# Storing the bias lines ahead of the last modulation pieces and the first weights, x as the first transfer, squares ahead of the line copy

## The reference

```python
x = x + pool_mixer(rmsnorm(x, norm_mixer[0]), pool_w[0], pool_scale[0])   # window means 2, 4, 8, 16, then a 256x256 product a group
x = x + swiglu(rmsnorm(x, norm_ffn[0]), w_gate_up[0], w_down[0])          # D_FF 2816
...
bias = bias_t[h_idx, bucket]                                              # relative bias of 16 heads, later of 8 more
mod = silu(c) @ ada_w + ada_b                                             # 1024 x 6144, used in the second block
```

## Time and profile before

| | us |
|---|---|
| median of 3 runs | 1400.96 |
| lowest and highest | 1398.17, 1401.15 |
| the profiled execution, its time | 1400.87 |
| its span in the trace | 1399.2 |
| TensorE busy in the span | 1330.1 (95%) |
| start of the first feed-forward product | 46.12 |

### The profile page before, as it was taken

How to read it: one execution, slowest core, us unless ns; L and a number is a source line. 1 busy time by engine, 2 the same in 40 slices (tenths; PEclk the granted TensorE clock), 3 DMA queues, 4 the chain that set the end, 5 groups by cost and what they waited for, 6 DMA issues and landing times.

```text
span 1399.2 us, 24627 instructions
## 1 busy us (share of the span) xinstructions
PE 1330.1 (95%) x10580; PEld 1013.9 (72%) x10580; DVE 678.1 (48%) x1075; ACT 510.9 (37%) x829; POOL 197.9 (14%) x96
## 2 busy tenths in 40 slices
PE   5899999999999999999997889999999999999997
PEld 3899999988899999799895789744444444444433
DVE  6665665666666665788985443511121112212113
ACT  2433433556533333467454442222222222222212
POOL 0000000000000000376781663000000000000002
PEclk9999999999999999999999999999999999999999
DMA  9965455745455336452316035349999999999994
GB/s 370 408 271 185 176 185 217 302 130 215 168 182 188 148 123 231 193 215 96 138 46 271 3 118 225 122 193 423 423 426 426 423 428 426 422 428 424 422 426 174
DMA packets 37507, 363.43 MB, mean 260 GB/s; under 512 B 5027, under 2 KB 6179, under 8 KB 8740
## 3 DMA queue, kind: packets, MB, share of 16 engines
q1 hardware_dynamic: 36692, 359.56, 63.8%
q0 software_dynamic: 720, 2.46, 0.9%
HBM read 359.32 MB, written 2.69 MB: 259 GB/s over the span
## 4 chain that ended last, share of the span: by engine, by line
PE 82%; DVE 8%; ACT 3%; DMA 3%; POOL 2%; issue 1%; SPq 0%; DVEq 0%; POOLq 0%; ACTq 0%
PE banks L1289 16%; PE banks L715 13%; PE banks L717 13%; PE banks L716 13%; PE banks L1314 8%; PE banks L1240 4%; PE banks L1249 4%; DMA bias_line<-scr 2%; POOL slot_lo L627 2%; PE banks L693 1%; PE banks L704 1%; PE banks L1255 1%; DMA scr<-bias_line 1%; PE banks L1063 1%; DVE ring L2077 1%
## 5 line engine op out<-in xcount | busy, mean ns | idle before, releaser
L715 PE MATMUL banks<-h_hi,gu_hi 128*128 128x256 f32 x704 | 199.5, 283 | 0.0
L717 PE MATMUL banks<-h_hi,slot_lo 128*128 128x256 f32 x704 | 199.2, 283 | 0.0
L716 PE MATMUL banks<-h_lo,gu_hi 128*128 128x256 f32 x704 | 199.2, 283 | 0.0
L717 PE MATMUL banks<-slot_lo,slot_lo 128*128 128x256 f32 x480 | 136.3, 284 | 0.0
L715 PEld LDWEIGHTS banks<-h_hi,gu_hi 128*128 128x128 f32 x704 | 135.2, 192 | 0.7 <-DVE slot_lo L1759 0.5
L716 PEld LDWEIGHTS banks<-h_lo,gu_hi 128*128 128x128 f32 x704 | 135.2, 192 | 0.0
L717 PEld LDWEIGHTS banks<-h_hi,slot_lo 128*128 128x128 f32 x704 | 135.2, 192 | 0.0
L2313 DVE TENSOR_TENSOR out_lo<-banks,out_hi 128x512 fp32r<-128x512 f32 x62 | 42.9, 692 | 185.0 <-ACT out_hi L1701 185.0
L1314 PE MATMUL banks<-ring,scr 128*64 128x512 f32 x512 | 116.9, 598 | 1.9 <-ACT scr L1695 1.9
L1289 PE MATMUL banks<-ring,scr 128*64 128x512 f32 x512 | 112.6, 592 | 0.0
L1289 PE MATMUL banks<-ring 128*64 128x512 f32 x512 | 112.6, 592 | 0.0
(11 more groups left out here) (420 smaller groups left out, 2985.3 us busy)
## 6 DMA issues: line engine op xcount, KB each, us to landing
ring<-experts SPq DMA_DIRECT2D x64, 2048.0 KB, 10.9
ring<-ws SPq DMA_DIRECT2D x77, 1536.0 KB, 7.2
ring<-experts SPq DMA_DIRECT2D x64, 1024.0 KB, 11.0
ring<-ada SPq DMA_DIRECT2D x16, 1536.0 KB, 7.0
ring<-experts SPq DMA_DIRECT2D x1, 3072.0 KB, 10.1
scr<-bias_line POOLq DMA_DIRECT2D x4, 512.0 KB, 8.0
bias_line<-scr SPq DMA_DIRECT2D x1, 1536.0 KB
x<-xT SPq DMA_DIRECT2D x1, 1024.0 KB, 5.3
```

Of the source, the lines that this page charges most:

```text
L715: nc.tensor.matmul(out, hi, move_hi, start=start, stop=False, skip_group_check=True)
L716: nc.tensor.matmul(out, hi, move_lo, start=False, stop=False, skip_group_check=True)
L717: return nc.tensor.matmul(out, lo, move_hi, start=False, stop=stop, skip_group_check=True)
```

## The change

```diff
@@ sync @@
+            sp.dma_start(x[:], xT).then_inc(x_loaded, 16)
+            sp.dma_start(vecs[:], vec).then_inc(vec_loaded, 16)
             sp.dma_start(sel_sb[0:BUCKETS + 1, :], selector).then_inc(sel_loaded, 16)
             sp.dma_start(relw[:], rel).then_inc(sel_loaded, 16)
-            sp.dma_start(vecs[:], vec).then_inc(vec_loaded, 16)
-            sp.dma_start(x[:], xT).then_inc(x_loaded, 16)
             sp.dma_start(icnt, inv_count).then_inc(pool_loaded, 16)
...
             sp.dma_start(poolw, pool_w).then_inc(pool_loaded, 16)
+            sp.wait_ge(line_copied, 1)
+            heads = HEADS_1 + HEADS_2
+            sp.dma_start(bias_line, line_sb[0:heads, :].unsqueeze(1).broadcast_to([heads, SHIFTS, 2 * T])).then_inc(line_stored, 16)
             load_ada(2)
             load_ada(3)
             load(0)
-            sp.wait_ge(line_copied, 1)
-            heads = HEADS_1 + HEADS_2
             sp.dma_start(con[:], consts).then_inc(const_loaded, 16)
-            sp.dma_start(bias_line, line_sb[0:heads, :].unsqueeze(1).broadcast_to([heads, SHIFTS, 2 * T])).then_inc(line_stored, 16)
@@ tensor @@
             pe.wait_ge(ones_ready, 1)
+            norm_sum(0)
             pe.wait_ge(sel_loaded, 32)
             nc.tensor.matmul(B[7][0:HEADS_1 + HEADS_2, :], relw[:], sel_sb[0:BUCKETS + 1, :], start=True, stop=True).then_inc(pe_step, 1)
-            norm_sum(0)
             pe.wait_ge(csil_ready, 2)
@@ scalar @@
             act.wait_ge(ones_ready, 1)
+            nc.scalar.activation(small[:, 61:62], eps, ACT.Sigmoid)
             act.wait_ge(vec_loaded, 16)
             nc.scalar.activation(csig, vecs[:, VEC["c"][0]:VEC["c"][1]], ACT.Sigmoid).then_inc(csil_ready, 1)
             load_table(ACT.Sqrt)
+            norm_squares(0)
             act.wait_ge(pe_step, 1)
             nc.scalar.activation(line_sb[0:HEADS_1 + HEADS_2, :], B[7][0:HEADS_1 + HEADS_2, :], ACT.Copy).then_inc(line_copied, 1)
-            norm_squares(0)
@@ vector @@
             dve.wait_ge(pool_loaded, 32)
+            dve.wait_ge(pe_step, 1)
             for g in range(4):
```

## The result

The changed kernel takes 1406.41 us (median of 5 runs, 1405.06 to 1407.48) against 1400.04 (1398.17 to 1401.15): a ratio of 1.0039 with a 95% interval of 1.0020 to 1.0058. It is slower, by 3 to 8 us, and by more than the 2.4 that I forecast. The median lies 0.4 us above my range of 1398.0 to 1406.0; the ratio on the median before gives 1405.5, just inside it. The profiled execution took 1405.06, with a span of 1403.4 (before: 1399.2), the fastest of the five.

What follows compares the result with a forecast made beforehand. TensorE, busy 95% of the span, was taken as the bound, so a shift at the head passes to the end. +3.5 us (`h_lo` later) - 1.1 (clock) = +2.4 on 1400.87 gives 1403.3; range 1398.0 to 1406.0.

Steps and rivals of the forecast that it cites:

- the mechanism of the path: At the head: the 3.67 us store wait goes, but late `ws` 0 delays split and `h_lo`, by +3.5 us.
- the store's 8.9 us for its followers: SyncE's queue: 12.6 us between landings of `con` and `ws` 1, less 3.7 for `ws` 1, leaves 8.9.
- x's 0.5: Head of the queue: issuing x 1.25 us earlier brings the transfers behind it 0.5 us forward.
- an estimate by 12 of the 16 engines: The store, spread over 12 DMA engines at 12/16 of full rate, would take 4.9 us; sum then -1.6.
- the clock: TensorE's last sum before the feed-forward part runs at 2.4 GHz instead of 1.2: -1.1 us.
- The queue may stand empty for 0 to 1 us. I take 0.: SyncE's wait ahead of the store: issue at 15.7 to 16.6, earlier transfers landed by 18.0, gap taken as 0.
- that 8.9 us are the store's price whatever its issue: Store moved ahead of four transfers: they land 8.9 - 0.5 = 8.4 us later, `ws` 0 at 38.0.
- the likeliest outcome: Whole kernel: 0.47 on the same time, 0.35 on slower, 0.18 on faster; about 0.2% (2.8 us) counts as change.
- My slow rival: SyncE's wait empties the queue for 1 us and no clock gain comes: +4.5 us, 1405.4; chance 10%.
- The two rivals on the fast side: Store costs only its bytes, 1398.1 to 1399.2, 17%; `ws` 0 and `ada` 2 come in time anyway, 1396.8, 13%.
- The squares: ScalarE's squares begin at about 8.2 against 7.46, 0.7 us late, covered by the later `ws` 0.

Runs made afterwards that it cites:

- the run on ScalarE's queue: Kernel before with the late wait, and the store issued by ScalarE right behind its line copy: 1397.57 us against 1398.98, ratio 0.9987.
- the store back: Changed kernel with the store and its wait back behind `ws` 0 and `con`: 1397.21 us against 1399.07, ratio 0.9989.
- the late wait: Kernel before with only VectorE's wait for the store moved from in front of `h_lo` to behind `add_modulation`: 1395.57 us against 1399.07, ratio 0.9970.
- `vecs` first: Changed kernel with the late wait, the store in its old place and `vecs` issued before x: 1395.79 us against 1398.98, ratio 0.9977.
- the store behind `ws` 1: Kernel before with the late wait and the store also behind `ws` 1: 1394.83 us against 1398.98, ratio 0.9973; second run 1395.27, ratio 0.9982.
- the early copy: Changed kernel with selector's product and line copy back ahead of the norm's sum and squares: 1402.27 us against 1398.98, ratio 1.0023.
- two stores: Changed kernel with the store cut in two, 16 heads in the new place, 8 behind `con`: 1405.55 us against 1399.07, ratio 1.0043.

## Why the prediction was right or wrong

- **Right: the mechanism of the path.** The wait for the store went, and `ws` 0 became what is late, by the path that I named: split, second half, `h_lo`. The distance from the landing of `ws` 0 to `h_lo` was 45.13 - 40.98 = 4.15 (predicted 4.3), from `h_lo` to the first product 6.40. All landings stood in the order of issue.
- **Right: the store's 8.9 us for its followers**, from two landings. The run with only the store moved shows it to a tenth, the run on ScalarE's queue shows that it is not the bytes alone. Without x's 0.5 the sum is +2.9, and that run measured +2.9 at the first product. The prediction also set an estimate by 12 of the 16 engines, 4.9 us, beside the 8.9, and kept only its sign. The trace agrees with the twelve: in the changed kernel, from 19 to 25 us, 466 rows at 0.15 us are the time of 11.7 engines, and the transfer behind uses the rest. What the estimate lacked was that a row itself takes longer.
- **Right: the clock**, -1.0 against -1.1. The last sum ran at 2.4 GHz in 1.13 us. The level there was up in every later profile as well. One stage earlier it is not to be foreseen: in nine of the twelve profiles the clock was low in part or all of the pool products. They took 10.2 us with the store back, 10.0 with the late wait and with `vecs` first, 9.5 in the second run of the store behind `ws` 1, 8.8 with only the store moved, 8.7 in the changed kernel's second profile, 7.5 to 7.9 in its first, with the early copy and with two stores, and 7.14 in the other three.
- **Wrong: "The queue may stand empty for 0 to 1 us. I take 0."** It idled for 1.06, and for 0.40 in the second profile. SyncE issued at 16.14, inside my 15.7 to 16.6, while the pool weights landed at 17.6, 0.4 ahead of my 18.0, and their last packets were through by 17.2. From its issue to its first rows the store needed 1.6 us of the 3 that I had allowed.
- **Wrong: that 8.9 us are the store's price whatever its issue.** This is the term that failed most. It is 8.9 for a store issued 8 us or more ahead of its turn. Issued onto a queue that runs dry, it is 33.5 - 17.6 - 3.7 = 12.2, of which 1.1 is the gap; the other 2.2 are slow rows from the start. The second profile gives 33.1 - 17.7 - 3.7 = 11.7, with 0.4 of gap and 2.4 of slow rows. The trace of before showed the high rate and then the low one in the store's stretch, and I took only the mean. Together: predicted +8.4 for `ws` 0, measured 8.4 + 1.1 + 2.2 - 0.4 (x first gave 0.9, not 0.5) = 11.3.
- **Wrong, therefore, the likeliest outcome.** I had 0.47 on no change and 0.35 on slower; the time is 0.39% over. My slow rival had the empty queue as its cause, rightly, but let the clock's gain lapse instead of the rows' speed, and so its 1405.4 came near for half a reason. My range reached up to the measured time only for the sake of this rival, so that part of the hit is luck.
- The two rivals on the fast side are refuted for SyncE's queue: `ws` 0 landed at neither 32.8 nor in time.
- The squares began at 7.89 (predicted 8.2), 0.4 us late instead of 0.7, and were covered, as said.

## What to carry to other kernels

Before a transfer is moved ahead of others, price it by what it does to the landing of the one behind it, not by its bytes: here 8.9 us against 3.7, and 12.2 where it was issued late. A wait can sometimes be moved at no cost where the transfer can't, as here; ask which memory it guards, and who writes there first. A transfer that waits for a computed value belongs behind enough queued work that the queue never runs dry at it.

## What the runs showed of the hardware that was not expected

- The store of 32 copies of each line (2 KB rows) goes on at over 400 GB/s, its neighbours' reads among them, for about 2 us if it was issued 8 us or more ahead of its turn (401 to 442 in two runs), then falls to 256 to 281. Issued onto an emptying queue it runs at 193 to 276 for its first eight microseconds (two profiles).
- By the packets of the traces, a row takes either 0.084 us or about 0.15. In the eight profiles in which SyncE issued the whole store 8 us or more ahead of its turn, 409 to 518 of the 768 rows were fast, with no more of them at 26 us ahead than at 11. In the two profiles of the changed kernel 4 and 21 were.
- With 16 lines instead of 24 it ran at 98 to 106 GB/s, 0.297 us a row, and took as long.
- Behind such a store SyncE's next issues take longer: 2.61 us for two and 2.25 for one in the changed kernel, where 1.08 and 0.49 were the lengths before. The store need not be under way for that: with only the store moved, the issues took 5.64 and 3.70, from 8.18 on, and the store's first rows came near 18.
- The pool products take 7.1 us or up to 10.2, with a granted clock of 1.00 or 0.50, and the same kernel shows both: 7.14 and 9.54 in the two profiles of the store behind `ws` 1. TensorE had idled 1.80 us ahead of the first and 1.73 ahead of the second.
